# Where a head pair's value products stand in two attention layers of a fused four-layer kernel

## The chip, the cores and the metric

The kernel is one program on one core of a Trainium2 chip. TensorE (PE in the profile), VectorE (DVE), ScalarE (ACT), GpSimd (POOL) and SyncE (SP) each run their own list of instructions in order and meet only at semaphores. The metric is device time of one execution in microseconds (us), the median over runs. Lower is better.

## The reference

256 tokens of width 1024 pass through two blocks of two layers each. The second layer (chunk band attention, 16 heads of 64) and the fourth and last layer (a forgetting attention over 16 more heads, with 16 meta tokens ahead of the sequence) are the ones that the change touches. All in fp32:

```python
# second layer: every chunk of 64 attends to itself and the chunks left of it
qkv = u @ w_qkv                      # 1024 -> 3 x 1024
scores = q k^T / 8 + rel_bias
p = softmax(where(valid, scores, -inf))
h = h + (p v) @ w_out
...
# last layer: keys and queries are RMS-normed per head, a decay is added
k, v, fl = split(h_n @ w_kv);  q = rms_norm(h_m @ w_q)
s = q k^T / 8 + (c_q - c_k)          # c: cumulated log forget gate
p = softmax(where(causal, s, -inf))
h = h + (p v) @ w_out
```

Every attention is followed by a feed-forward layer; those, and the first and third layer, are left as they are.

## The kernel before

**Weights.** All weights stream from memory in blocks of 128 x 1024 (512 KB) through a ring of four slots. Each block is split into two fp32r halves: ScalarE rounds it (`whi`, L320), VectorE takes the rest (`wlo`, L325), three blocks ahead of TensorE. TensorE then multiplies a block in 24 matmuls, eight chunks of three products (L341, L342, L343; `unit_mm`). Nearly the whole kernel is such blocks one behind the other.

**A head pair.** In the second layer (`band_*`) and the last (`fox_*`) the 16 heads go in 8 pairs. Stage `s` of a hand-written software pipeline holds two weight blocks, which give the keys and queries of pair `s`, and between them the attention work of earlier pairs:

- `pair_turn_pe(s-2)`: transposes of the probabilities (L835 to L839) into PSUM banks; ScalarE copies them to `probT` (`turned_act`, L851), and in the last layer also the meta part to `probT_meta` (L853).
- `scores(s-1)`: L912, L915. VectorE adds the bias and takes the maximum (L959), ScalarE the exponential (L968), VectorE scales (L857, L861).
- `values(p)`: value products of pair `p` (`pair_values_pe`: L927 in the last layer only, L930, L932) from `probT`. ScalarE rounds the result (`out_hi`, L844), VectorE takes the rest (`out_lo`, L867), as input of the output projection.

`probT` and the PSUM bank of the value products exist once. So `turned_act` of pair p+1 waits until the value products of pair p are done, and `values(p+1)` waits for `out_lo` of pair p:

```python
# turned_act
act.wait_ge(pt_ready, hd + 1)
if hd // 2 > 0:
    act.wait_ge(o_ready, hd // 2)
# pair_values_pe
if pr > 0:
    pe.wait_ge(o_lo, pr)
pe.wait_ge(pt_copied, a.head0 + 2 * s + 2)
```

**In the last layer there is more around it.** Each block's result `yb` is multiplied out of PSUM (VectorE, `unit`, L1306), squared (ScalarE, `square`, L1229), summed over the head by one more matmul into the block's own bank (`stat`, L1164), and turned into a factor (ScalarE, `rms`, L1237 and L1240). `unit(2*s+2)` on TensorE waits for `rms(2*s)`, since it overwrites that bank, and `stat(2*s+1)` stands inside it, behind five of its eight chunks. ScalarE's list for stage s is: split, `rms(2s-1)`, `out_hi`, `square(2s)`, the copies of `turned_act`, the exponentials, `rms(2s)`, split, `square(2s+1)`. VectorE evacuates block 2s+1 only behind its own half of that second split.

**Behind the loop** (the tail) come the last two value blocks (`values_unit` or `unit(BAND_V[..])`), the last turns and scores, late transposes of values (`late_turn`, L752 to L754, copied by L759 and L761), and the first output projection blocks (`out_part_pe`) around the last turn and value products.

Of the kernel before, what the change touches and what calls it, by code (L numbers as in the profile page):

```python
# [157 lines left out]
def program(nc, stream, xT, metaT, gains, consts, relh, decay, out):  # L158
    with ExitStack() as ctx:
# [681 lines left out]
        def out_hi(act, a, s):  # L841
            pr = a.head0 // 2 + s
            act.wait_ge(o_ready, pr + 1)
            act.activation(ahi[:, a.chunk0 + s, a.cols], a.obank[:, 0:256], ACT.Copy).then_inc(o_hi, 1)  # L844
# [152 lines left out]
        def band_pe(pe):  # L997
            a, n0, b0, v0, last = band, START["bqk"], BSTART["bqk"], VFIRST["bv"], band.pairs - 1

            def unit(i, inside=None):  # L1000
                b = b0 + i
                pe.wait_ge(evac, b - 1)
                unit_mm(pe, At(n0 + i), bank[2 + b % 2][:, 0:SEQ], uhi, ulo, FIRST, inside=inside)

            def last_early_turn():
                v = LATE["bv"] - 1
                dst = bank[5 + v % 2]
                pe.wait_ge(evac, b0)
                pe.wait_ge(v_stored, v0 + v)
                pe.transpose(dst[:, 0:128], yb[:, v % 4, META:META + 128], const("ident"))  # L1010
                pe.transpose(dst[:, 128:256], yb[:, v % 4, META + 128:T], const("ident")).then_inc(v_turned, 1)

            def late_turn(v):
                late_turn_pe(pe, "bv", v, b0 + BAND_V[v], yb[:, v % 4, :])

            def scores(s):
                pe.wait_ge(evac, b0 + 2 * s + 2)
                if s == 0:
                    pe.wait_ge(v_stored, v0 + LATE["bv"])
                pair_scores_pe(pe, a, s)  # L1020

            def values(s):
                pe.wait_ge(v_stored, v0 + s + 1)
                pair_values_pe(pe, a, s)

            for s in range(a.pairs):
                unit(2 * s, inside=None if s else last_early_turn)
                if s >= 2:
                    pair_turn_pe(pe, a, s - 2)
                if s >= 1:  # L1030
                    scores(s - 1)
                unit(2 * s + 1)
                if s >= 2:
                    values(s - 2)
            unit(BAND_V[6])
            pair_turn_pe(pe, a, last - 1)
            scores(last)
            late_turn(6)
            unit(BAND_V[7])
            values(last - 1)  # L1040
            late_turn(7)
            out_part_pe(pe, "out1", a, 0, 0, 6, FIRST)
            pair_turn_pe(pe, a, last)
            out_part_pe(pe, "out1", a, 1, 0, 7, FIRST)
            values(last)
            out_part_pe(pe, "out1", a, 2, 0, 7, FIRST)
            for j, c in enumerate((6, 7, 7)):
                out_part_pe(pe, "out1", a, j, c, DC, FIRST)
            out_part_pe(pe, "out1", a, 3, 0, DC, FIRST)
            out_rest_pe(pe, "out1", FIRST)  # L1050

        def band_act(act, link):
            a, n0, b0, last = band, START["bqk"], BSTART["bqk"], band.pairs - 1

            def split(i):
                split_hi(act, At(n0 + i + AHEAD))

            def last_early_store():
                v = LATE["bv"] - 1
                act.wait_ge(v_turned, VFIRST["bv"] + v + 1)  # L1060
                act.activation(v_cols(At(v), 0, 256, P), bank[5 + v % 2][:, 0:256], ACT.Copy).then_inc(v_stored, 1)

            def late_store(v):
                late_store_act(act, "bv", v, b0 + BAND_V[v])

            for s in range(a.pairs):
                split(2 * s)
                if s == 0:
                    last_early_store()
                if s >= 3:  # L1070
                    out_hi(act, a, s - 3)
                if s >= 2:
                    pair_turned_act(act, a, s - 2)
                if s >= 1:
                    pair_biased_exp_act(act, a, s - 1)
                    if s + 1 < a.pairs:
                        act.dma_start(relb[:, (s + 1) % 2, :, :], relh[s + 1]).then_inc(rel_loaded[(s + 1) % 2], 16)
                split(2 * s + 1)
            split(BAND_V[6])
            out_hi(act, a, last - 2)  # L1080
            pair_turned_act(act, a, last - 1)
            late_store(6)
            pair_biased_exp_act(act, a, last)
            split(BAND_V[7])
            out_hi(act, a, last - 1)
            late_store(7)
            split_hi(act, At(START["out1"] + AHEAD))
            pair_turned_act(act, a, last)
            out_hi(act, a, last)

        def band_dve(dve, link):
            a, n0, b0, last = band, START["bqk"], BSTART["bqk"], band.pairs - 1

            def unit(j, first, scale):
                dve.wait_ge(w_used, n0 + j + 1)
                dve.scalar_tensor_tensor(out=chunk_at(first, At(j // 2), FIRST), in0=bank[2 + (b0 + j) % 2][:, 0:SEQ], scalar=scale,
                                         in1=rstd[:, 0, FIRST], op0=ALU.mult, op1=ALU.mult).then_inc(evac, 1)

            def values_unit(v):
                i = BAND_V[v]  # L1100
                dve.wait_ge(w_used, n0 + i + 1)
                dve.tensor_tensor(yb[:, v % 4, FIRST], bank[2 + (b0 + i) % 2][:, 0:SEQ], rstd[:, 0, FIRST], ALU.mult).then_inc(evac, 1)

            def split(i):
                split_lo(dve, At(n0 + i + AHEAD))

            for s in range(a.pairs):
                split(2 * s)
                if s >= 3:
                    out_lo(dve, a, s - 3)  # L1110
                unit(2 * s, Q0, HD ** -0.5)
                if s >= 1:
                    pair_softmax_dve(dve, link, a, s - 1)
                split(2 * s + 1)
                unit(2 * s + 1, K0, 1.0)
            split(BAND_V[6])
            out_lo(dve, a, last - 2)
            values_unit(6)
            for i in (2 * last, 2 * last + 1):
                biased_max_dve(dve, a, i)  # L1120
            values_unit(7)
            split(BAND_V[7])
            pair_scale_dve(dve, link, a, last)
            out_lo(dve, a, last - 1)
            split_lo(dve, At(START["out1"] + AHEAD))
            out_lo(dve, a, last)
# [11 lines left out]
        def fox_pe(pe):  # L1138
# [50 lines left out]
            for s in range(a.pairs):  # L1189
                if s == 0:  # L1190
                    unit(0, inside=last_early_turn)
                    unit(1, inside=lambda: stat(0))
                    values_unit(5, 1, inside=lambda: stat(1))
                    continue
                unit(2 * s, inside=(lambda s=s: stat(2 * s - 1)) if s > 1 else None)
                if s >= 2:
                    pair_turn_pe(pe, a, s - 2)
                else:
                    late_turn(5)
                scores(s - 1)  # L1200
                stat(2 * s)
                unit(2 * s + 1)
                if s >= 2:
                    values(s - 2)
            values_unit(6, 2 * last + 1, inside=lambda: stat(2 * last + 1))
            pair_turn_pe(pe, a, last - 1)
            scores(last)
            late_turn(6)
            values_unit(7, 2 * last + 2)
            values(last - 1)  # L1210
# [11 lines left out]
        def fox_act(act, link):  # L1222
# [19 lines left out]
            def split(i):  # L1242
                split_hi(act, At(n0 + i + AHEAD))
# [22 lines left out]
            for s in range(1, a.pairs):  # L1266
                split(fox_at(2 * s))
                if s >= 2:
                    rms(2 * s - 1)
                if s >= 3:  # L1270
                    out_hi(act, a, s - 3)
                square(2 * s)
                if s >= 2:
                    pair_turned_act(act, a, s - 2)
# [7 lines left out]
                square(2 * s + 1)  # L1282
            split(FOX_V[6])
            rms(2 * last + 1)
            out_hi(act, a, last - 2)
            pair_turned_act(act, a, last - 1)
            late_store(6)
            pair_biased_exp_act(act, a, last)
            split(FOX_V[7])
            out_hi(act, a, last - 1)  # L1290
            late_store(7)
# [4 lines left out]
        def fox_dve(dve, link):  # L1296
# [35 lines left out]
            for s in range(1, a.pairs):  # L1332
                split(fox_at(2 * s))
                if s >= 2:
                    normed(2 * s - 1)
                if s >= 3:
                    out_lo(dve, a, s - 3)
                unit(2 * s)
                pair_softmax_dve(dve, link, a, s - 1)
                normed(2 * s)  # L1340
# [4 lines left out]
                    unit(2 * s + 1)  # L1345
            split(FOX_V[6])
            normed(2 * last + 1)
            out_lo(dve, a, last - 2)
            values_unit(6)
            for i in (2 * last, 2 * last + 1):  # L1350
                biased_max_dve(dve, a, i)
            values_unit(7)
            split(FOX_V[7])
            pair_scale_dve(dve, link, a, last)
# [1337 lines left out]
```

## Time and profile before

| | |
|---|---|
| runs | 1282.69, 1283.51, 1284.3 us; median 1283.51 |
| profiled execution | span 1282.5 us from first to last instruction (its own time is not given; the median lies 1.0 us above the span) |
| TensorE busy | 98% of the span |
| VectorE, ScalarE, GpSimd busy | 63%, 58%, 29% |
| granted TensorE clock | 0.998 of full speed, mean |
| second layer's attention | about 340 to 422 us of the span |
| last layer's attention | about 980 to 1079 us |

Times in the trace count from the span's start. A matmul's row has its start and its modelled length; since matmuls are pipelined, the distance between two starts is what one costs. A row's bracket is the idle time of the engine ahead of it, and what ended that.

### The profile page before, as it was taken

The page shows a single profiled execution, that of the slowest core. Times are in us where ns is not written, and L with a number is a line of the kernel's source. Part 1 is how long each engine was busy: PE and PEld are TensorE (multiplying, and loading weights), DVE is VectorE, ACT ScalarE, POOL GpSimd, SP SyncE. Part 2 cuts the span into 40 slices and gives each one's busy share as a digit, 9 for nine tenths or more (in the row PEclk, how much of TensorE's full clock was granted, in tenths as well). Part 3 has the DMA queues.
Part 4 walks back from the last instruction along what each step waited for, and adds up shares of the span by engine and source line. Part 5 has one row for each costly group of instructions (what it writes and reads, how often), then busy time and mean ns, then how long its engine had stood idle before and what let it go on. Part 6 is the DMA issues. An engine that isn't in the chain of part 4 may idle for free.

```text
span 1282.5 us, 28401 instructions
## 1 busy us (share of the span) xinstructions
PE 1261.1 (98%) x10337; PEld 1215.3 (95%) x10337; DVE 809.9 (63%) x1422; ACT 738.5 (58%) x1375; POOL 376.8 (29%) x416
## 2 busy tenths in 40 slices
PE   6999999999999999999999899999999999999999
PEld 6988999999988999999989599999999889999999
DVE  5687755556576655557699875554547665755544
ACT  6576766654456566665566854443436776544433
POOL 2011344411000244431243127770100220677100
PEclk9999999999999999999999999999999999999999
DMA  7542555566654465566455045556555443655664
GB/s 265 177 136 87 190 186 184 183 208 200 215 174 151 153 193 181 192 194 205 154 185 171 9 150 181 178 170 191 168 177 181 151 139 100 192 186 182 196 191 154
DMA packets 66503, 220.55 MB, mean 172 GB/s; under 512 B 9312, under 2 KB 13808, under 8 KB 66288
## 3 DMA queue, kind: packets, MB, share of 16 engines
q1 hardware_dynamic: 64080, 212.77, 52.1%
q10 hardware_dynamic: 2336, 6.58, 1.7%
q8 instruction: 60, 0.98, 0.3%
q14 instruction: 27, 0.22, 0.1%
HBM read 215.61 MB, written 1.08 MB: 169 GB/s over the span
## 4 chain that ended last, share of the span: by engine, by line
PE 77%; issue 10%; POOL 5%; DVE 4%; ACT 3%; DMA 0%; POOLq 0%; ACTq 0%; SPq 0%; DVEq 0%
PE bank L341 23%; PE bank L343 22%; PE bank L342 22%; POOL scratch L581 1%; POOL scratch L583 1%; DVE wlo L325 1%; PE bank L930 1%; PE bank L915 1%; POOL alo L585 1%; ACT whi L320 1%; DVE scratch L571 1%; ACT ahi L556 1%; PE bank L912 1%; ACT prob L968 1%; PE bank L355 1%
## 5 line engine op out<-in xcount | busy, mean ns | idle before, releaser
L325 DVE TENSOR_TENSOR wlo<-raw,whi 128x1024 fp32r<-128x1024 f32 (+1 forms) x394 | 484.0, 1229 | 162.0 <-ACT whi L320 161.2
L341 PE MATMUL bank<-uhi,whi 128*128 128x256 f32 (+1 forms) x1848 | 532.8, 288 | 11.4 <-DVE wlo L325 10.7
L343 PE MATMUL bank<-uhi,wlo 128*128 128x256 f32 (+1 forms) x1848 | 525.0, 284 | 0.0
L342 PE MATMUL bank<-ulo,whi 128*128 128x256 f32 (+1 forms) x1848 | 524.3, 284 | 0.0
L320 ACT ACTIVATE whi<-raw 128x1024 fp32r<-128x1024 f32 (+1 forms) x394 | 410.6, 1045 | 183.7 <-PE bank L343 175.4
L341 PEld LDWEIGHTS bank<-uhi,whi 128*128 128x128 f32 x1848 | 349.8, 189 | 19.4 <-issue 17.1
L343 PEld LDWEIGHTS bank<-uhi,wlo 128*128 128x128 f32 x1848 | 350.1, 189 | 0.0
L342 PEld LDWEIGHTS bank<-ulo,whi 128*128 128x128 f32 x1848 | 348.7, 189 | 0.6
L341 PE MATMUL bank<-ahi,whi 128*128 128x256 f32 (+1 forms) x1168 | 332.9, 285 | 0.4 <-DVE wlo L325 0.4
L343 PE MATMUL bank<-ahi,wlo 128*128 128x256 f32 (+1 forms) x1168 | 330.6, 283 | 0.0
L342 PE MATMUL bank<-alo,whi 128*128 128x256 f32 (+1 forms) x1168 | 330.3, 283 | 0.0
L341 PEld LDWEIGHTS bank<-ahi,whi 128*128 128x128 f32 x1168 | 220.3, 189 | 2.6 <-issue 1.2
L343 PEld LDWEIGHTS bank<-ahi,wlo 128*128 128x128 f32 x1168 | 220.6, 189 | 0.0
L342 PEld LDWEIGHTS bank<-alo,whi 128*128 128x128 f32 x1168 | 219.8, 188 | 0.3
L619 POOL TENSOR_TENSOR scratch<-scratch 128x272 f32<-128x272 f32 (+1 forms) x64 | 97.0, 1515 | 25.3 <-DVE scratch L608 25.3
L422 POOL TENSOR_TENSOR sum_of_squares<-sum_of_squares,scratch 128x256 f32<-128x256 f32 (+1 forms) x48 | 42.9, 893 | 180.4 <-ACT scratch L399 176.6
L598 ACT ACTIVATE ahi<-scratch 128x272 f32 (+1 forms) x64 | 27.2, 425 | 92.8 <-DVE scratch L608 92.8
L608 DVE SCALAR_TENSOR_TENSOR scratch<-bank,rstd 128x272 f32<-128x272 f32 (+1 forms) x64 | 27.7, 433 | 82.5 <-PE bank L343 80.4
L422 POOL TENSOR_TENSOR sum_of_squares<-scratch 128x256 f32<-128x256 f32 (+1 forms) x8 | 6.9, 858 | 244.4 <-ACT scratch L399 237.5
L571 DVE TENSOR_TENSOR scratch<-bank,scratch 128x256 f32<-128x256 f32 x44 | 18.7, 425 | 85.6 <-POOL scratch L583 85.6
L585 POOL TENSOR_TENSOR alo<-scratch,ahi 128x256 f32 x44 | 43.2, 982 | 53.1 <-ACT ahi L556 53.1
L581 POOL TENSOR_TENSOR scratch<-scratch 128x256 f32<-128x256 f32 x44 | 32.6, 741 | 86.8 <-ACT scratch L553 86.8
(286 smaller groups left out, 1245.8 us busy)
## 6 DMA issues: line engine op xcount, KB each, us to landing
raw<-stream SPq DMA_DIRECT2D x394, 512.0 KB, 3.6
scratch<-decay ACTq DMA_DIRECT2D x8, 416.0 KB, 3.7
scratch<-relh ACTq DMA_DIRECT2D x8, 384.0 KB, 3.4
scratch<-scratch SPq DMA_DIRECT2D x68, 34.0 KB, 2.5
constants<-consts SPq DMA_DIRECT2D x1, 1296.0 KB, 11.1
h<-xT SPq DMA_DIRECT2D x4, 256.0 KB, 5.7
out<-h SPq DMA_DIRECT2D x8, 128.0 KB, 3.5
scratch<-scratch SPq DMA_DIRECT2D x16, 16.0 KB, 2.9
```

The lines of the kernel that those rows point to most:

```text
L320: act.activation(whi[:, s, 0:w], raw[:, s, 0:w], ACT.Copy).then_inc(w_hi, 1)
L325: dve.tensor_tensor(wlo[:, s, 0:w], raw[:, s, 0:w], whi[:, s, 0:w].bitcast(F32), ALU.subtract).then_inc(w_lo, 1)
L341: pe.matmul(dst, hi, a, start=first and i == 0, stop=False)
L342: pe.matmul(dst, hi, b, start=False, stop=False)
L343: mm = pe.matmul(dst, lo, a, start=False, stop=last and i == chunks - 1)
L422: pool.tensor_tensor(acc[:, cols], first, sq_all[:, m, cols], ALU.add).then_inc(acc_done, 1)
L571: dve.tensor_tensor(mval[:, j, cols], bank[(b0 + 2 * j + 1).mod(4)][:, 0:width(cols)], tgate[:, j, cols], ALU.mult).then_inc(evac, 1)
L581: pool.tensor_tensor(tgate[:, j, cols], gate[:, j, cols], egate[:, j, cols], ALU.mult).then_inc(t_ready, 1)
L585: pool.tensor_tensor(hidden_at(alo_t, At(j, it, 2), cols), mval[:, j, cols], hidden_at(ahi_t, At(j, it, 2), cols).bitcast(F32), ALU.subtra ...
L598: act.activation(hidden_at(ahi_t, At(j, it, 4), cols), gate[:, j % 2, cols], ACT.Square).then_inc(a_hi, 1)
L608: dve.scalar_tensor_tensor(out=gate[:, j % 2, cols], in0=bank[(b0 + j).mod(4)][:, 0:width(cols)], scalar=0.0, in1=rstd[:, 0, cols], op0=AL ...
L619: pool.tensor_tensor(mval[:, j % 2, cols], gate[:, j % 2, cols], gate[:, j % 2, cols], ALU.mult).then_inc(a_sq, 1)
```

## The change

Value products of a pair move on TensorE within the stages: `values(s-2)`, which stood behind the second block of stage s, is done instead in stage s+1 as `values(s-3)`, directly behind the scores there. In the tail `values(last-2)` moves behind `scores(last)`. Six of the eight pairs move in each of the two layers; the last two stay. ScalarE's `out_hi` and VectorE's `out_lo` of a pair follow one stage later. No instruction is added or removed. The same edits are made in `band_*` and `fox_*`; those of `fox_*` are:

```diff
 # fox_pe (band_pe alike, without stat)
                 scores(s - 1)
+                if s >= 3:
+                    values(s - 3)
                 stat(2 * s)
                 unit(2 * s + 1)
-                if s >= 2:
-                    values(s - 2)
             values_unit(6, 2 * last + 1, inside=lambda: stat(2 * last + 1))
             pair_turn_pe(pe, a, last - 1)
             scores(last)
+            values(last - 2)
             late_turn(6)
             values_unit(7, 2 * last + 2)
             values(last - 1)
 # fox_act (band_act alike)
-                if s >= 3:
-                    out_hi(act, a, s - 3)
+                if s >= 4:
+                    out_hi(act, a, s - 4)
...
-            out_hi(act, a, last - 2)
+            out_hi(act, a, last - 3)
             pair_turned_act(act, a, last - 1)
             late_store(6)
             pair_biased_exp_act(act, a, last)
+            out_hi(act, a, last - 2)
             split(FOX_V[7])
             out_hi(act, a, last - 1)
 # fox_dve (band_dve alike)
-                if s >= 3:
-                    out_lo(dve, a, s - 3)
+                if s >= 4:
+                    out_lo(dve, a, s - 4)
...
-            out_lo(dve, a, last - 2)
+            out_lo(dve, a, last - 3)
             values_unit(6)
             for i in (2 * last, 2 * last + 1):
                 biased_max_dve(dve, a, i)
+            out_lo(dve, a, last - 2)
             values_unit(7)
```

On TensorE, in stage 5 of the last layer, before: the scores (`scratch` holds queries and keys) and what follows them.

```order
L912 MATMUL bank<-scratch 128x144 [waits s_max,y_done]
L912 MATMUL bank<-scratch 128x144
L915 MATMUL bank<-scratch 128x272 x2
L1164 MATMUL bank<-scratch,constants 128x272 [waits y_sq]
L341 MATMUL bank<-ahi,whi 128x256 [waits w_lo,y_rstd,evacuated]
```

The end of the same stage, before:

```order
L343 MATMUL bank<-ahi,wlo 128x256
L927 MATMUL bank<-probT_meta,scratch 64x256 [waits pt_copied,meta_copied,o_lo,v_stored]
L927 MATMUL bank<-probT_meta,scratch 64x256
L930 MATMUL bank<-probT,scratch 64x256 x2
L932 MATMUL bank<-probT,scratch 64x128 x2
L341 MATMUL bank<-uhi,whi 128x272 [waits w_lo,y_rstd,evacuated]
```

Now (lines behind L1029 are a few higher: L1167 is L1164 of before):

```order
L912 MATMUL bank<-scratch 128x144 [waits s_max,y_done]
L912 MATMUL bank<-scratch 128x144
L915 MATMUL bank<-scratch 128x272 x2
L927 MATMUL bank<-probT_meta,scratch 64x256 [waits pt_copied,meta_copied,o_lo,v_stored]
L927 MATMUL bank<-probT_meta,scratch 64x256
L930 MATMUL bank<-probT,scratch 64x256 x2
L932 MATMUL bank<-probT,scratch 64x128 x2
L1167 MATMUL bank<-scratch,constants 128x272 [waits y_sq]
L341 MATMUL bank<-ahi,whi 128x256 [waits w_lo,y_rstd,evacuated]
```

The value products (of an earlier pair) have moved from between two blocks to between the scores and the sum of squares, with all their waits.

On ScalarE, in the tail of the last layer, before:

```order
L851 ACTIVATE probT<-bank 128x384 [waits o_ready,pt_ready] x2
L853 ACTIVATE probT_meta<-bank 16x512
L759 ACTIVATE scratch<-bank 16x128 [waits v_turned]
L761 ACTIVATE scratch<-bank 128x256 [waits late_meta]
L968 ACTIVATE prob,softmax_columns<-prob,softmax_columns 128x144 [waits s_max]
L968 ACTIVATE prob,softmax_columns<-prob,softmax_columns 128x272
L968 ACTIVATE prob,softmax_columns<-prob,softmax_columns 128x144 [waits s_max]
L968 ACTIVATE prob,softmax_columns<-prob,softmax_columns 128x272
L320 ACTIVATE whi<-raw 128x1024 [waits w_used,w_loaded1]
L844 ACTIVATE ahi<-bank 128x256 [waits o_ready]
```

And now:

```order
L851 ACTIVATE probT<-bank 128x384 [waits o_ready,pt_ready] x2
L853 ACTIVATE probT_meta<-bank 16x512
L759 ACTIVATE scratch<-bank 16x128 [waits v_turned]
L761 ACTIVATE scratch<-bank 128x256 [waits late_meta]
L968 ACTIVATE prob,softmax_columns<-prob,softmax_columns 128x144 [waits s_max]
L968 ACTIVATE prob,softmax_columns<-prob,softmax_columns 128x272
L968 ACTIVATE prob,softmax_columns<-prob,softmax_columns 128x144 [waits s_max]
L968 ACTIVATE prob,softmax_columns<-prob,softmax_columns 128x272
L844 ACTIVATE ahi<-bank 128x256 [waits o_ready]
L320 ACTIVATE whi<-raw 128x1024 [waits w_used,w_loaded1]
L844 ACTIVATE ahi<-bank 128x256 [waits o_ready]
```

One more rounding of value products (L844, pair 5's) has come between the last exponentials and the split.

## Rows read from the trace of the kernel before

**Rows 1.** The page: busy time of an engine, its share of the span, instructions.
```profile
PE 1261.1 (98%) x10337; PEld 1215.3 (95%) x10337; DVE 809.9 (63%) x1422; ACT 738.5 (58%) x1375; POOL 376.8 (29%) x416
```

**Rows 2.** Timeline of TensorE, last layer, stages 4 and 5: start, length, line.
```profile
1019.97 0.70 PE L1164 MATMUL bank<-scratch,constants 128*128 128x256 f32 x2
...
1023.17 0.62 PE L915 MATMUL bank<-scratch 64*128 64x272 f32 x4
1023.73 0.73 PE L1164 MATMUL bank<-scratch,constants 128*128 128x272 f32 x2
...
1027.01 0.28 PE L343 MATMUL bank<-ahi,wlo 128*128 128x256 f32 x1
1027.22 0.65 PE L927 MATMUL bank<-probT_meta,scratch 128*64 128x256 f32 x4
...
1028.13 0.39 PE L932 MATMUL bank<-probT,scratch 128*64 128x128 f32 x4
1028.45 0.39 PE L341 MATMUL bank<-uhi,whi 128*128 128x272 f32 x1
1028.68 0.29 PE L342 MATMUL bank<-ulo,whi 128*128 128x272 f32 x1
1028.80 0.28 PE L343 MATMUL bank<-uhi,wlo 128*128 128x272 f32 x1
...
1030.57 0.70 PE L1164 MATMUL bank<-scratch,constants 128*128 128x256 f32 x2
```

**Rows 3.** Timeline of TensorE in the third layer, scores followed by value products.
```profile
724.52 0.60 PE L915 MATMUL bank<-scratch 64*128 64x256 f32 x4
725.05 0.65 PE L930 MATMUL bank<-probT,scratch 128*64 128x256 f32 x4
```

**Rows 4.** Timeline of ScalarE, last layer, stages 4 and 5.
```profile
1023.57 0.85 ACT L851 ACTIVATE probT<-bank 128x384 f32<-128x384 f32 x2
...
1024.79 0.40 ACT L968 ACTIVATE prob<-prob,softmax_columns 128x144 f32<-128x144 f32 x1
...
1027.10 0.43 ACT L1240 ACTIVATE scratch<-log_mean 128x272 f32<-128x272 f32 x1
1027.43 1.04 ACT L320 ACTIVATE whi<-raw 128x1024 fp32r<-128x1024 f32 x1
1030.10 0.42 ACT L1229 ACTIVATE scratch<-scratch 128x256 f32<-128x256 f32 x1 [1.63 <-DVE scratch L1306]
```

**Rows 5.** Timeline of VectorE, last layer: the halves of two blocks' split.
```profile
1028.51 1.22 DVE L325 TENSOR_TENSOR wlo<-raw,whi 128x1024 fp32r<-128x1024 f32 x1 [0.44 <-ACT whi L320]
...
1031.50 1.36 DVE L325 TENSOR_TENSOR wlo<-raw,whi 128x1024 fp32r<-128x1024 f32 x1 [1.43 <-ACT whi L320]
```

**Rows 6.** Who waited for whom, 345 to 425 us: total, times, longest.
```profile
ACT probT L851 <- PE bank L839: 17.6, 8, 2.5
```

**Rows 7.** Timeline of TensorE, tails of the second and the last layer.
```profile
411.36 0.33 PE L753 MATMUL bank<-constants,scratch 128*128 128x128 f32 x1
...
414.56 0.65 PE L930 MATMUL bank<-probT,scratch 128*64 128x256 f32 x4
...
1066.71 0.28 PE L752 MATMUL bank<-constants,scratch 128*16 128x128 f32 x1
...
1070.15 0.65 PE L927 MATMUL bank<-probT_meta,scratch 128*64 128x256 f32 x4
```

**Rows 8.** Timeline of ScalarE, tail of the last layer.
```profile
1067.24 0.27 ACT L759 ACTIVATE scratch<-bank 16x128 f32<-16x128 f32 x1 [0.37 <-PE bank L754]
...
1067.82 0.41 ACT L968 ACTIVATE prob<-prob,softmax_columns 128x144 f32<-128x144 f32 x1
...
1069.62 1.04 ACT L320 ACTIVATE whi<-raw 128x1024 fp32r<-128x1024 f32 x1
```

**Rows 9.** All instructions of one line: shortest, median, longest in ns (L844; L867).
```profile
L844 ACT ACTIVATE ahi<-bank x28: 357/368/387, 76.7 to 1078.8; 128x256 fp32r<-128x256 f32 x28
...
L867 DVE TENSOR_TENSOR alo<-bank,ahi x28: 412/417/426, 78.6 to 1079.3; 128x256 fp32r<-128x256 f32 x28
```

More of the change, by code:

```diff
@@ L1200, in fox_pe @@
                 scores(s - 1)
+                if s >= 3:
+                    values(s - 3)
                 stat(2 * s)
                 unit(2 * s + 1)
-                if s >= 2:
-                    values(s - 2)
             values_unit(6, 2 * last + 1, inside=lambda: stat(2 * last + 1))
@@ L1207, in fox_pe @@
             scores(last)
+            values(last - 2)
             late_turn(6)
@@ L1269, in fox_act @@
                     rms(2 * s - 1)
-                if s >= 3:
-                    out_hi(act, a, s - 3)
+                if s >= 4:
+                    out_hi(act, a, s - 4)
                 square(2 * s)
@@ L1284, in fox_act @@
             rms(2 * last + 1)
-            out_hi(act, a, last - 2)
+            out_hi(act, a, last - 3)
             pair_turned_act(act, a, last - 1)
@@ L1288, in fox_act @@
             pair_biased_exp_act(act, a, last)
+            out_hi(act, a, last - 2)
             split(FOX_V[7])
@@ L1335, in fox_dve @@
                     normed(2 * s - 1)
-                if s >= 3:
-                    out_lo(dve, a, s - 3)
+                if s >= 4:
+                    out_lo(dve, a, s - 4)
                 unit(2 * s)
@@ L1347, in fox_dve @@
             normed(2 * last + 1)
-            out_lo(dve, a, last - 2)
+            out_lo(dve, a, last - 3)
             values_unit(6)
@@ L1351, in fox_dve @@
                 biased_max_dve(dve, a, i)
+            out_lo(dve, a, last - 2)
             values_unit(7)
```

## Prediction

> **What bounds the kernel now.** I read the page first, then the timelines of TensorE, ScalarE and VectorE through one stage of each of the two layers, then who waited for whom. The page says that TensorE is busy for 98% of the span [rows 1], so time goes down only if TensorE gets less to do or fewer gaps, and goes up by whatever makes it wait. The reader is to see two things in the timelines.
>
> In the last layer one stage takes 10.60 us, from the `stat` of one odd block at 1019.97 to that of the next at 1030.57 [rows 2], with almost no gap on TensorE. But a second chain is nearly as long. Follow stage 4 on ScalarE: the copies to `probT` start at 1023.57, the exponentials at 1024.79, `rms(2s)` ends at 1027.10 + 0.43 = 1027.53, and the split stands directly behind it at 1027.43 [rows 4]. VectorE waits for that split and does its half at 1028.51 for 1.22 us [rows 5], only then evacuates the odd block, and ScalarE, idle for 1.63 us and released by that evacuation (L1306), squares at 1030.10 and ends at 1030.52 [rows 4]. TensorE starts the `stat` at 1030.57, 0.05 later [rows 2]. So from the copies to that `stat` nothing is idle for a reason of its own: 1030.57 - 1023.57 = 7.00 us, all chain. TensorE comes to the `stat` at about the same moment; the chain is late by some 0.1 us already.
>
> In the second layer the same copies have room: they wait for TensorE 8 times, 17.6 us in all [rows 6], there is no `rms` and no `stat`, and no block waits on that part of ScalarE's list.
>
> **What the change removes on TensorE.** Two rows in sequence normally lie 0.12 us apart (1028.68 to 1028.80). Into the value products it is 0.21 (1027.01 to 1027.22), out of them the first product of the block costs 0.23 (1028.45 to 1028.68) [rows 2]. Rows of 64 x 128 or 128 x 64 tiles thus cost 0.09 going in and 0.11 coming out. Behind the scores, TensorE is in small tiles already and has to come out once anyway. From scores to what follows is 0.56 in the last layer (1023.17 to 1023.73) [rows 2], and from scores straight to value products, which the third layer shows, 0.53 (with 256 columns where the other has 272) [rows 3]. So that step costs the same, and a moved pair saves 0.09 + 0.10 = 0.19 us. Six pairs in two layers: 12 x 0.19 = 2.3 us, the most that the change can give. The bounds of this term are 0 and 0.20 for each.
>
> The row that I weighed a rule against is the step from scores to value products, 128-column tiles of 64 rows to 64-column tiles of 128 rows [rows 3]. The Trainium skill, "TensorEngine Tiling (Array Packing)", section Key Properties, says that changing the tiling mode (not just the tile) drains the TensorE. By that rule scores and value products are two modes as well, so that of four drains in a stage three stay and one goes: at 0.1 us each that would be 12 x 0.1 = 1.2 us in place of 2.3, and a band layer that gains 0.6 less. The rows show two such steps gone and no new one, so the sum goes by 0.19.
>
> **What it adds in the last layer.** `turned_act` of pair s-2 waits for the value products of pair s-3. Before, these were done a stage half earlier; now they stand behind turns and scores of the same stage. Put in numbers of stage 4: value products would start where `stat(2s)` did, 1023.73. They take 1.23 us (1027.22 to 1028.45), and their last group ends 0.07 behind the start of what follows (1028.13 + 0.39 = 1028.52) [rows 2]. So they end at 1023.73 + 1.30 = 1025.03, and with 0.04 for the semaphore the copies start at 1025.07 instead of 1023.57 [rows 4]: 1.50 us later. Queued behind them on ScalarE are the exponentials, `rms(2s)`, on which block 2s+2 waits, the split, and the square, and behind VectorE's half of the split the evacuation. As the chain has no slack, `stat(2s+1)` starts 1.50 us later too, at 1032.07. TensorE would first wait for `rms(2s)` at the start of block 2s+2 (by some 0.7 us) and for the rest at the `stat`; together it is one delay.
>
> This is a closed loop: from `stat` to the next value products 3.76 us of TensorE work (1019.97 to 1023.73) [rows 2], 1.34 until the copies start, 7.00 until the next `stat`. That is 12.10 us against 10.60, +1.50 for a stage. It begins with stage 3, whose late copies hit the `stat` in stage 4, and holds for the stages 3 to 7: 5 x 1.50 = 7.5 us. The first `stat` of that row (stage 3) comes about 0.1 earlier than before, since no products stand ahead of it: 7.4 us. In these five periods before, five pairs' products were done, and now too; but the sixth, which was done ahead of the first `stat` before, is now done behind the last: +1.23 us.
>
> **The tail of the last layer.** Pair 5's products now follow the last scores. Clock of before: they start at 1066.71 [rows 7], end at 68.01, and the copies start at 68.05. To the exponentials it is 1.22 as in the loop [rows 4] plus 0.58 for the two late copies (1067.24 to 1067.82), which gives 69.85; exponentials take 1.80 (1067.82 to 1069.62) [rows 8]: 71.65. Then `out_hi` 0.37 and `out_lo` 0.42 [rows 9], with two semaphores 72.5. Value products of pair 6 wait for this `out_lo`; TensorE is there at 1070.15 [rows 7] + 1.23 = 71.4. A new wait of 1.1 us. What comes behind it (last turn, which needs VectorE's scaling) has room for it.
>
> **The second layer.** No stall in the loop: its copies start about 2 us later, within their 17.6 us of waiting [rows 6]. In the tail the same new wait: TensorE's products there are 0.75 us (1.23 without the four L927 at 0.12), start at 411.36 and end at 412.2 [rows 7]; copies 0.85 [rows 4], one late copy 0.3, exponentials 1.8, `out_hi` and `out_lo` 0.86 give 416.0, against 414.56 [rows 7] + 0.75 = 415.3. Of 0.7 I take 0.6, as TensorE's exit from small tiles is not paid there twice. The layer: -6 x 0.19 + 0.6 = -0.5 us. In the last layer the saving of 6 x 0.19 vanishes in TensorE's waiting.
>
> **Sum.** 7.4 + 1.2 + 1.1 - 0.5 = 9.2 us. The profile gives a span of 1282.5 us and no time of that execution; the median of the runs is 1.0 above it. 1283.5 + 9.2 = 1292.7 us.
>
> One cost I can't fix: a split of VectorE took 1.36 instead of 1.22 [rows 5] while GpSimd added causal masks. The split is part of the chain now, so each such meeting is paid. Bounds: none (0.6 us less than the sum, the part of it that is in the span of before), or one in every stage (2.4 us more). I leave it as before. The Trainium skill, "GPSIMD Engine Reference", section Specifications, has GpSimd's SBUF interfaces shared with VectorE, with contention for instructions that read two SBUF inputs, which the split does; the slower row agrees.
>
> **The rivals.**
> - *The copies' delay finds slack, and only the tile steps count* (the other side). For it: in the second layer it is so, and ScalarE is busy 58% only. Against it: the 1.63 us of idle time lies inside the chain and ends by VectorE's evacuation, so it is no slack. It gives 1283.5 - 2.3 = 1281.2 us. It decides from a slack of 1.5 us between copies and `stat`; the rows show none. Chance 0.04.
> - *Only the `rms` wait bites*: VectorE evacuates the odd block without being held by the split, and a stage costs 0.7 - 0.2 = 0.5 us. 5 x 0.5 + 1.2 + 1.1 - 0.5 = 4.3, or 1287.8 us. Against it: the evacuation stands behind that split in VectorE's list. Chance 0.06.
> - *The tails have room* that I did not see: 9.2 - 1.7 = 7.5, or 1291.0 us. Chance 0.1, within the forecast's own range.
> - *GpSimd meets the chain in every stage*: 1295.1 us. Chance 0.1.
>
> **How the numbers follow.** My forecast has 0.7 at 1292.7; the two neighbours with 0.1 each lie at 1291.0 and 1295.1. The range 1289.0 to 1295.5 holds these and leaves out the first two rivals. Within 0.2% (2.6 us, about what a measurement of this kernel can tell from no change) lies the first rival alone; slower by more than that is everything else. Faster by over 0.2% would need more than the whole 2.3 us of tile steps: 0.01.
>
> **What the changed profile would show.** Value products 0.53 to 0.56 behind the start of L915, with no wait. In the last layer: `stat` of odd blocks 12.1 us apart, a PE wait for ScalarE's `rms` of 0.7 at the start of even blocks and for its square of 1.0 at the `stat`, copies (L851) released by L932 instead of being ready. In both tails L927 or L930 of pair 6 waiting for `out_lo` (L867), 1.1 and 0.6 us. In the second layer stages of 8.15 us, with no wait. Stages of 10.4 in the last layer would prove me wrong, and so would the copies starting ahead of L932's end.

## The result, and the profile after

The changed kernel takes 1293.65 us (median of 5 runs, 1292.19 to 1294.8) against 1283.51 before: ratio 1.0077, 95% interval 1.0065 to 1.0089. Forecast were 1292.7 us and a range of 1289.0 to 1295.5. In every run the time lies 1.7 to 1.9 us above the span, so the profiled execution of before, with its span of 1282.5, was near that kernel's highest time of 1284.3, while the one profiled here was the lowest of the five (1292.19 us, span 1290.3). The two spans therefore differ by less than the medians do; below I compare lengths within a layer, which don't depend on that.

The page, with the same columns as [rows 1]: TensorE has the same number of instructions and 1.2 us less busy time in a span that is 7.8 us longer. The added time is waiting.

```profile
PE 1259.9 (98%) x10337; PEld 1214.7 (94%) x10337; DVE 809.4 (63%) x1422; ACT 738.0 (57%) x1375; POOL 378.0 (29%) x416
```

The timeline of TensorE through one stage of the last layer, the counterpart of [rows 2] (L1167 is L1164 of before):

```profile
1019.19 0.70 PE L1167 MATMUL bank<-scratch,constants 128*128 128x256 f32 x2 [0.81 <-ACT scratch L1233]
...
1022.39 0.62 PE L915 MATMUL bank<-scratch 64*128 64x272 f32 x4
1022.95 0.65 PE L927 MATMUL bank<-probT_meta,scratch 128*64 128x256 f32 x4
1023.43 0.60 PE L930 MATMUL bank<-probT,scratch 128*64 128x256 f32 x4
1023.86 0.39 PE L932 MATMUL bank<-probT,scratch 128*64 128x128 f32 x4
1024.18 0.73 PE L1167 MATMUL bank<-scratch,constants 128*128 128x272 f32 x2
...
1028.42 0.36 PE L341 MATMUL bank<-uhi,whi 128*128 128x272 f32 x1 [0.68 <-issue]
...
1031.65 0.70 PE L1167 MATMUL bank<-scratch,constants 128*128 128x256 f32 x2 [1.10 <-ACT scratch L1233]
...
1043.83 0.70 PE L1167 MATMUL bank<-scratch,constants 128*128 128x256 f32 x2 [0.82 <-ACT scratch L1233]
...
1053.06 0.36 PE L341 MATMUL bank<-uhi,whi 128*128 128x272 f32 x1 [0.68 <-issue]
...
1056.01 0.70 PE L1167 MATMUL bank<-scratch,constants 128*128 128x256 f32 x2 [0.82 <-ACT scratch L1233]
...
1068.19 0.70 PE L1167 MATMUL bank<-scratch,constants 128*128 128x256 f32 x2 [0.81 <-ACT scratch L1233]
```

The value products stand 0.56 behind L915, without a wait. A stage is 1056.01 - 1043.83 = 12.18 us; one of the five is 12.46. Each has a wait at the start of the even block (0.68) and one at the `stat` (0.81 or 0.82, and 1.10 in the long stage), which the square (L1233) ends.

ScalarE in the same stage, the counterpart of [rows 4]:

```profile
1022.46 0.43 ACT L1233 ACTIVATE scratch<-scratch 128x272 f32<-128x272 f32 x1 [1.29 <-DVE scratch L1311]
1024.36 0.49 ACT L851 ACTIVATE probT<-bank 128x384 f32<-128x384 f32 x1 [1.47 <-PE bank L932]
...
1025.59 0.40 ACT L968 ACTIVATE prob<-prob,softmax_columns 128x144 f32<-128x144 f32 x1
...
1027.89 0.43 ACT L1244 ACTIVATE scratch<-log_mean 128x272 f32<-128x272 f32 x1
1028.23 1.04 ACT L320 ACTIVATE whi<-raw 128x1024 fp32r<-128x1024 f32 x1
1031.18 0.42 ACT L1233 ACTIVATE scratch<-scratch 128x256 f32<-128x256 f32 x1 [1.91 <-DVE scratch L1311]
```

Read it with the rows above: ScalarE was free for the copies (L851) at 1022.89 and waits 1.47 us for the last value product, L932. The `rms` ends at 1028.32 and TensorE's block starts at 1028.42. The square ends at 1031.60 and the `stat` starts at 1031.65. Each link is the one that the prediction named. One is longer than it had: the row of L932 ends at 1023.86 + 0.39 = 1024.25, and the copies start 0.11 behind that, not 0.04.

TensorE in both tails, the counterpart of [rows 7]; the bracket is the new wait:

```profile
413.03 0.65 PE L930 MATMUL bank<-probT,scratch 128*64 128x256 f32 x4 [0.61 <-issue]
...
1077.88 0.65 PE L927 MATMUL bank<-probT_meta,scratch 128*64 128x256 f32 x4 [1.19 <-issue]
```

The bracket names no engine; that it is `out_lo` (L867) is read from VectorE's timeline, where it ends at 1077.77:

```profile
1077.35 0.42 DVE L867 TENSOR_TENSOR alo<-bank,ahi 128x256 fp32r<-128x256 f32 x1 [4.04 <-ACT ahi L844]
```

In the second layer the stages got shorter. TensorE's scores of two stages in sequence, now with the products behind them:

```profile
399.65 0.60 PE L915 MATMUL bank<-scratch 64*128 64x256 f32 x4
400.18 0.65 PE L930 MATMUL bank<-probT,scratch 128*64 128x256 f32 x4
400.66 0.39 PE L932 MATMUL bank<-probT,scratch 128*64 128x128 f32 x4
400.98 0.39 PE L341 MATMUL bank<-uhi,whi 128*128 128x256 f32 x1
...
407.81 0.60 PE L915 MATMUL bank<-scratch 64*128 64x256 f32 x4
```

That is 8.16 us for a stage, without a wait; before it was 8.34 (L912 from 393.82 to 402.16).

### The profile page after: what moved, and what is told of

It is laid out like the page before. It is cut to its first block, busy times and chain, and to the rows that moved or that the text cites. A ratio compares the mean times of both kernels' runs of the same rounds, so it can differ in the third digit from the quotient of the medians.

```text
span 1290.3 us, 28401 instructions
## 1 busy us (share of the span) xinstructions
PE 1259.9 (98%) x10337; PEld 1214.7 (94%) x10337; DVE 809.4 (63%) x1422; ACT 738.0 (57%) x1375; POOL 378.0 (29%) x416
## 4 chain that ended last, share of the span: by engine, by line
PE 75%; issue 10%; POOL 5%; DVE 4%; ACT 4%; DMA 1%; POOLq 0%; ACTq 0%; SPq 0%; DVEq 0%
PE bank L341 22%; PE bank L343 22%; PE bank L342 21%; POOL scratch L581 1%; POOL scratch L583 1%; ACT prob L968 1%; PE bank L930 1%; DVE wlo L325 1%; PE bank L915 1%; POOL alo L585 1%; ACT whi L320 1%; PE bank L912 1%; DVE scratch L571 1%; ACT ahi L556 1%; PE bank L355 1%
```

## The experiments

Theory: the loss is the delay of the copies to `probT`, which wait for value products that now stand late, in a layer where a chain without slack hangs on these copies. Rivals: the order on TensorE itself costs the time (tile steps, the wait for `out_lo`), in both layers; or the delay finds slack and something else is behind the loss. Two lengths go with each run, taken from its trace on TensorE: of the second layer from the first scores (L912) to the last L930, and of the last layer from the first `stat` with 256 columns to the last L932. Before: 67.89 and 91.11 us. After: 67.51 and 101.23. The ratios are to runs of the kernel before that were taken again beside each group of experiments (medians 1283.38 us for e1 to e4, 1283.39 for e5 to e8, 1283.83 for e9 and e10).

**One layer at a time.** e1 has the change in `band_*` only, e2 in `fox_*` only.

> The move in the second layer alone; the last layer as before. My theory (copies to probT delayed; they have room in this layer): stages of 8.15 us instead of 8.34, a wait of 0.6 us for pair 5's out_lo in the tail, in all 0.5 us less than before: 1283.0. The rival (the new neighbours on TensorE cost time wherever they stand) expects about 4 to 5 us more: 1288.

> The move in the last layer alone; the second layer as before. My theory: the whole loss is here, five stages of 12.2 us for 10.6, 1.2 for the displaced products and 1.2 in the tail: 10 us more than before, 1293.5. The rival (both layers pay alike): about 1288.

e1: 1283.3 us, ratio 1.0000 (0.9991 to 1.0009); lengths 67.48 and 91.12. e2: 1293.85, ratio 1.0083 (1.0069 to 1.0097); lengths 67.89 and 101.70. All of the loss is in the last layer. The second layer wins 0.4 us by its trace, which is less than the times can show. The last layer of e2 has the same program as that of the changed kernel and is 0.5 us longer: three of its five stages are long (12.42, 12.49 and 12.38), where the changed kernel has one.

**The waiting for the copies taken away, with TensorE's order kept.**

```diff
+        probTA2 = c_t[:, CCOL["cos"][0]:CCOL["cos"][0] + 512]
+        probT2 = c_t[:, CCOL["cosm"][0]:CCOL["cosm"][0] + 768].rearrange("p (b n) -> p b n", b=2)
...
+        def pt_of(a, s):
+            return probT2 if a.two and s % 2 else a.pt
...
-            if hd // 2 > 0:
-                act.wait_ge(o_ready, hd // 2)
+            free = hd // 2 - (1 if a.two and i >= 2 else 0)
+            if free > 0:
+                act.wait_ge(o_ready, free)
```

> The whole change, but probT and probT_meta exist twice (pairs alternate; the second ones lie over constants that are no longer used), so that the copies of a pair no longer wait for the value products of the pair ahead. TensorE's order is that of the change. My theory: the copies start as early as before, the last layer's stages are back at 10.6 us, and no out_lo is late in the tails. What stays there is 1.2 us for the sixth pair's products, now behind the last stat, against 1.1 us won in the second layer: 1283.5, as before. The rival (the order on TensorE itself, its tile steps or the wait for out_lo, costs the time): 1292 or more, as with the change.

The value products read the second buffer too (not shown), and GpSimd clears the second `probT_meta` once, ahead of the last layer. 1285.33 us, ratio 1.0009 (1.0000 to 1.0018); lengths 67.06 and 92.20. With the same order of matmuls as the changed kernel, the last layer is 9.0 us shorter. Its copies no longer wait, and a stage (L1174 is the `stat` here) is back at 10.59:

```profile
1041.87 0.70 PE L1174 MATMUL bank<-scratch,constants 128*128 128x256 f32 x2
...
1052.46 0.70 PE L1174 MATMUL bank<-scratch,constants 128*128 128x256 f32 x2
```

```profile
1045.13 0.43 ACT L1240 ACTIVATE scratch<-scratch 128x272 f32<-128x272 f32 x1 [1.29 <-DVE scratch L1318]
1045.47 0.85 ACT L858 ACTIVATE probT<-bank 128x384 f32<-128x384 f32 x2
```

That decides against the order on TensorE. Two parts of the expectation failed. Both tails keep a short wait, read as the one for `out_lo` (0.16 and 0.33 us), for `out_hi` of pair 5 stands behind the exponentials however early those are. And the time is 1.8 us above the 1283.5 that I expected, while the two lengths together are only 0.3 above those of before. Most of the rest stands ahead of both layers: in this trace the second layer's first scores start at 354.55 us, before at 353.10. Over the twelve traces of this case that start lies between 351.93 and 354.55, though no edit touches the first layer; what moves it was not looked into.

**The delay of the copies alone, in the kernel before.**

```diff
                 if s >= 2:
+                    act.wait_ge(y_stat, r0 + 2 * s + 1)
                     pair_turned_act(act, a, s - 2)
```

> The kernel before, with TensorE's order untouched; in the last layer the copies to probT in the stages 2 to 7 wait in addition for stat(2s), which makes them 0.9 us later. My theory (copies to stat is a chain without slack): each of six stages gets 0.9 us longer, 5.6 in all: 1289.1. The rival (that delay finds slack and the loss is from the order on TensorE): no change, 1283.5.

1290.25 us, ratio 1.0051 (1.0037 to 1.0065); lengths 67.90 and 96.93, so 5.8 us more than before in the last layer. TensorE's list is that of before; its undisturbed stages are now 11.54 us, 0.94 longer. ScalarE's copies start 4.53 us behind the `stat` of the odd block (at 1022.34), where it was 3.60 before:

```profile
1026.87 0.87 ACT L851 ACTIVATE probT<-bank 128x384 f32<-128x384 f32 x2 [0.83 <-PE bank L1164]
```

A delay of 0.93 us of the copies goes into the stage in full. Together e3 and e4 take the cause away and put it in by itself.

**The chain shortened behind the copies.** VectorE evacuates the odd block ahead of its half of the split: e5 on the changed kernel, e6 on the kernel before.

```diff
-                if s == 1:
-                    unit(2 * s + 1)
+                unit(2 * s + 1)
                 split(fox_at(2 * s + 1))
-                if s > 1:
-                    unit(2 * s + 1)
```

> The whole change, and in the last layer VectorE evacuates block 2s+1 ahead of its half of the second split instead of behind it. That takes the split out of the chain from the copies to stat(2s+1) and leaves the wait for rms(2s) at the start of block 2s+2. My theory: the wait of 0.8 to 1.1 us at the stat goes, the one of 0.7 at the block stays; five stages of 11.4 instead of 12.2 us: 1289.4. The rival (the rms wait alone set the stage, the stat wait was cover): 1293.5, no change.

> The kernel before with the same edit on VectorE alone. My theory: the chain was some 0.12 us too late at the stat in five stages already, and more where GpSimd met it; 0.6 to 1.0 us less than before: 1282.7. The rival (TensorE alone set those stages): 1283.5.

e5: 1287.26 us, ratio 1.0033 (1.0021 to 1.0045); last layer 94.49. The wait at the `stat` is gone and the one at the block stays (0.70 to 0.73):

```profile
1027.03 0.36 PE L341 MATMUL bank<-uhi,whi 128*128 128x272 f32 x1 [0.73 <-issue]
...
1028.99 0.59 PE L1167 MATMUL bank<-scratch,constants 128*128 128x256 f32 x2
```

The direction is right and the size is off by 2.1 us: stages are 11.10 us, not 11.4, since I subtracted only the bracket, and the first `stat`, a stage ahead of the five, also had a wait of 0.82 that I had forgotten. With the `rms` wait alone, this is the prediction's second rival made real: 11.10 is its 10.60 + 0.5. e6: 1282.21, ratio 0.9990 (0.9981 to 0.9999); last layer 89.39, stages 10.36 instead of 10.60. The chain was holding the kernel before too, and by more than I expected (0.6 to 1.0 us): the layer is 1.7 us shorter, the time 1.3 by its ratio.

**Both, to see the tile steps.** e7 is the change with two buffers and the early evacuation; e8 is e1 with `out_hi` of pair 5 ahead of the last exponentials:

```diff
+            out_hi(act, a, last - 2)
             pair_biased_exp_act(act, a, last)
-            out_hi(act, a, last - 2)
```

> The whole change with two probT buffers (as e3) and VectorE's early evacuation (as e5). My theory: now neither the copies nor the split hold a stat, TensorE bounds both layers, and the 0.19 us of tile steps for each of twelve pairs show: 1283.5 - 2.3 - 0.6 = 1280.6. The rival (tile steps are hidden by other waits): 1282.7, as e6.

> The move in the second layer alone (as e1), with pair 5's out_hi on ScalarE ahead of the last exponentials instead of behind them. My theory: the wait for out_lo in the tail (0.6 us) goes, TensorE keeps all of 6 x 0.19: 1282.4. The rival (the tail then waits for the scaling, which is later by the 0.37 us of out_hi): 1282.8.

e7: 1281.59 us, ratio 0.9985 (0.9975 to 0.9994); lengths 67.08 and 88.94, stages of 10.14 to 10.18 against 10.36 in e6. That is the 0.19 us of tile steps, now visible because no wait is left in the stages. By time e7 doesn't decide: it lies 1.0 us above the theory's 1280.6 and 1.1 below the rival's 1282.7. The stages decide for the theory. The tails' waits (0.16 and 0.34) are 0.5 us of what is missing. e8: 1282.74, ratio 0.9994 (0.9985 to 1.0003), unclear by time; second layer 67.08, 0.81 less than before. The wait for `out_lo` is gone, but the last turn now waits for VectorE's scaling, which ends at 416.55: the second head's first transpose stands 0.51 behind the first's instead of 0.32. Both sides were partly right.

```profile
416.10 0.27 PE L837 MATMUL bank<-constants,prob 128*128 128x128 f32 x1
...
416.61 0.33 PE L837 MATMUL bank<-constants,prob 128*128 128x128 f32 x1
```

**What beats both kernels.**

> e7 (whole change, two probT buffers, early evacuation) with pair 5's out_hi ahead of the last exponentials in both layers. My theory: the two short waits for out_lo that e7 still has in its tails (0.2 and 0.3 us) go, the last layer's stages stay at 10.2 us: 1281.2, 2.2 us less than before. The rival: the later exponentials cost as much at the last turn: 1281.6, as e7.

> No second buffer: the second layer as in e8 (products moved, early out_hi), the last layer as in e6 (products where they were before, early evacuation). The two gains should add, 0.8 us in the second layer and 1.7 in the last layer's stages: 1281.2. If they don't add: 1282.2, as e6.

e9: 1280.38 us, ratio 0.9977 (0.9968 to 0.9986); lengths 66.84 and 88.50, no wait of TensorE in either layer's attention that the timeline brackets. It has the lowest median of all versions, 0.8 us below what I expected and 1.2 below the rival's. Its TensorE in one stage of 10.14 us:

```profile
1037.50 0.59 PE L1174 MATMUL bank<-scratch,constants 128*128 128x256 f32 x2
...
1040.60 0.62 PE L922 MATMUL bank<-scratch 64*128 64x272 f32 x4
1041.15 0.65 PE L934 MATMUL bank<-constants,scratch 128*64 128x256 f32 x4
...
1047.64 0.59 PE L1174 MATMUL bank<-scratch,constants 128*128 128x256 f32 x2
```

e10: 1282.06, ratio 0.9986 (0.9977 to 0.9995); lengths 67.07 and 89.33. The two gains add in the trace (0.8 and 1.8, 2.6 us); the time shows 1.8 with an interval of 0.6 to 3.0. Its median is near the 1282.2 that stood for gains that don't add, so the time doesn't decide between the two, and only the lengths do.

## Why the prediction was right

- *The closed loop of the last layer* (1.50 us a stage, 7.5 in all): from the first `stat` of the row (1007.01) to the last (1068.19) it is 61.18 us, before 53.48. That is 7.7 more, and 1.58 for an undisturbed stage. The cause, the copies waiting for the products ahead of them, is shown by e3 and e4. By the parts, a stage is 3.76 us from `stat` to the value products, 1.41 until the copies start and 7.01 or 7.02 until the next `stat`, where the prediction had 3.76, 1.34 and 7.00. The part that was too small is the 0.04 from the end of L932 to the copies, which is 0.11.
- *The sixth pair's products, now behind the last `stat`* (1.23 us), and *the tail* (1.1): from the last `stat` to the last L932 it is 1086.14 - 1068.19 = 17.95 us, before 1078.41 - 1062.95 = 15.46. The 2.5 us are the two terms (2.3): the products take 1.24 (1071.94 to 1073.18), and pair 6's come 1.26 later behind `late_turn` than before, of which the bracket shows 1.19.
- *The second layer* (-0.5): -0.38 by its length. Six moves gain 1.05 us where nothing waits (e9's layer against that of before), 0.17 to 0.18 each instead of 0.19, and the tail's wait is 0.61 in its bracket. e7's stages against e6's show 0.20 each, where the other value that the prediction weighed was 0.1. In the last layer the prediction let the steps vanish in TensorE's waiting, and so it was until e7 took the waits away.
- *The sum* (9.2): 10.12 - 0.38 = 9.7 by the two lengths, 10.1 by the medians. The sum is 0.5 too low by the lengths: 0.2 in the loop, 0.2 in the tail and 0.1 in the second layer. In the loop 5 x 0.08 from the late copies is partly offset, since GpSimd's rows made one stage 0.3 longer here and one 0.6 longer before. That offset is luck of the profiled execution: in e2, with the same program in this layer, three stages were lengthened. The 0.4 between lengths and medians is within the spread of the runs.
- *The state before.* The prediction had the chain late by some 0.1 us at the `stat`. It cost 0.24 a stage (10.60 against e6's 10.36), for the two `stat` rows behind such a late arrival take 0.35 instead of 0.25 too. The sum doesn't use this number, so it wasn't hurt by it.
- *The rivals.* Slack in the chain and "only the `rms` wait" are out: the second is what e5 makes of the kernel, and it takes an edit on VectorE to get there. "The tails have room" is out by their two waits. GpSimd in every stage did not come true: it lengthened one stage of five (12.46 us), as in the kernel before (11.19 where the others have 10.60).

## What to carry to other kernels

Before work is moved on the busiest engine, look at what else its end releases: here no later work of TensorE waited for the value products directly, but they freed a buffer on which ScalarE waited with its whole list behind it. A loop that seems bound by one engine at 98% may have a second chain of the same length; 1.5 us of delay on that chain is worth eight times the 0.19 us of the step that is saved. Such a chain shows itself in other engines' brackets: ScalarE's idle 1.63 us ended by VectorE's evacuation, and ahead of that VectorE's half of the split had waited for ScalarE. Shortening the chain alone was not enough for this reordering (e5, 1287.26 us); with the second buffer as well it paid in the stages (e7), and with both tails put right in the time too (e9).

## What the runs showed of the hardware

Idle brackets understate a wait of TensorE. A stage of the changed kernel is 12.18 us and with the same matmuls and no wait 10.16 (e9), 2.0 apart, while its brackets add up to 0.68 + 0.81 = 1.5. The rest is in the rows. A product of 272 columns is shown 0.29 us long, though the next starts 0.13 behind it where nothing waits, so that each wait hides about 0.16. Behind a wait two `stat` rows take 0.35 (1031.65 to 1032.00) instead of the 0.25 that e5 shows without one (1028.99 to 1029.24), and the first row of a block takes 0.20 (1028.42 to 1028.62) instead of 0.13. That makes 2.0.

In these rows going into small tiles and coming out costs about 0.1 us each way. The step from 64 x 128 to 128 x 64 tiles costs as much as the one from 64 x 128 to whole tiles: it is 0.53 from L915 to L930 in the second layer, as in [rows 3], and in the kernel before, where a whole block followed L915 there, 0.52 (402.49 to 403.01). Whether that is more than staying in tiles of one kind these rows can't tell for L915; four rows of 256 columns that stay in 128 x 64 tiles take 0.43 (1023.43 to 1023.86). What a move saves is thus one way in and one way out.

Beside GpSimd's mask rows VectorE took longer in four stages of the changed kernel (there are none in the last one), mostly where it did not matter. The factor's product (L1323) took 0.63 to 0.76 us instead of 0.50, in front of a wait for ScalarE, and one split took 1.51. Lying beside them isn't enough: in three of the four stages the split of this chain lay inside the mask rows too (at 1017.13, with the rows from 1016.14 for 2.94) and took its usual 1.23. What decides was not tested. The long one:

```profile
1028.35 0.63 DVE L1323 SCALAR_TENSOR_TENSOR scratch<-scratch,gain_columns 128x272 f32<-128x272 f32 x1
1029.30 1.51 DVE L325 TENSOR_TENSOR wlo<-raw,whi 128x1024 fp32r<-128x1024 f32 x1 [0.32 <-ACT whi L320]
```

```profile
1028.23 2.89 POOL L983 TENSOR_TENSOR scratch<-scratch,constants 128x128 f32<-128x128 f32 x4 [9.16 <-DMA scratch<-decay]
```
